# The first norm row spread by four short products, and four instruction orders moved in the token mixers

## The reference, cut to what matters

```python
h = rms_norm(x, norm_mix_pre[l])
z = h @ w_in[l]
q_h, f_fw, f_bw, i_h, g_h, q_d, k_d, v_d, gate_a, gate_b = split(z)
a = hgrn2_mixer(q_h, f_fw, f_bw, i_h, g_h, lb[l], hgrn_gnorm[l])   # 4 heads, gated linear attention, both directions
b = diff_attention(q_d, k_d, v_d, ...)                              # 4 heads, softmax(q k) twice, rope, rms_norm
m = sigmoid(gate_a) * (a @ w_branch_a[l]) + sigmoid(gate_b) * (b @ w_branch_b[l])
x = x + rms_norm(m @ w_out[l], norm_mix_post[l])
x = x + rms_norm(conv_ffn(rms_norm(x, norm_ffn_pre[l]), ...), norm_ffn_post[l])
x = x + rms_norm(sigmoid(rms_unit(x) @ w_ple_gate[l]) * (p[l] @ w_ple[l]), norm_ple[l])
```

## Time and profile before

| what | value |
|---|---|
| median of 3 runs | 2416.17 us (2415.14 to 2419.05) |
| the profiled execution | 2415.63 us, its span 2413.7 us |
| PE busy | 2401.1 us, 99% |
| DVE busy | 1839.3 us, 76% |
| ACT busy | 1311.3 us, 54% |
| POOL busy | 197.1 us, 8% |
| HBM, mean over the span | 132 GB/s |

### The profile page before, as it was taken

How to read it: one execution, slowest core, us unless ns; L and a number is a source line. 1 busy time by engine, 2 the same in 40 slices (tenths; PEclk the granted TensorE clock), 3 DMA queues, 4 the chain that set the end, 5 groups by cost and what they waited for, 6 DMA issues and landing times.

```text
span 2413.7 us, 40388 instructions
## 1 busy us (share of the span) xinstructions
PE 2401.1 (99%) x16188; PEld 2241.4 (93%) x16188; DVE 1839.3 (76%) x2412; ACT 1311.3 (54%) x2022; POOL 197.1 (8%) x236
## 2 busy tenths in 40 slices
PE   9999999999999999999999999999999999999998
PEld 8999999998999999888889999999989999998887
DVE  7666788764888999978585568887649889999784
ACT  6445666542555556456464456664426555554563
POOL 1001011100200000003110011111001000000031
PEclk9999999999999999999999999999999999999999
DMA  5454444353323233733233544434443233346421
GB/s 178 136 175 141 137 146 136 126 181 133 103 89 92 83 97 121 289 123 122 98 131 129 186 136 141 138 129 143 159 150 105 65 90 93 104 164 241 160 89 62
DMA packets 284667, 320.97 MB, mean 133 GB/s; under 512 B 10433, under 2 KB 216769, under 8 KB 284482
## 3 DMA queue, kind: packets, MB, share of 16 engines
q1 hardware_dynamic: 211680, 171.39, 22.8%
q10 hardware_dynamic: 72802, 147.01, 16.8%
HBM read 253.08 MB, written 65.27 MB: 132 GB/s over the span
## 4 chain that ended last, share of the span: by engine, by line
PE 94%; DVE 3%; ACT 1%; issue 1%; DMA 0%; SPq 0%; DVEq 0%; ACTq 0%; POOLq 0%; POOL 0%
PE ps L909 23%; PE ps L1192 14%; PE ps L1397 13%; PE ps L1137 8%; PE ps L882 6%; PE ps L1503 5%; PE ps L1120 3%; PE ps L1366 3%; PE ps L1333 3%; PE ps L896 3%; PE ps L1252 3%; PE ps L961 1%; PE ps L1483 1%; PE ps L1109 1%; PE ps L1089 1%; PE ps L1018 1%
## 5 line engine op out<-in xcount | busy, mean ns | idle before, releaser
L2143 DVE TENSOR_TENSOR wlo<-raw,whi 128x1024 fp32r<-128x1024 f32 (+1 forms) x152 | 163.8, 1079 | 55.1 <-ACT whi L3165 55.1
L909 PE MATMUL ps<-hT_hi,whi 128*128 128x384 f32 x608 | 203.1, 334 | 0.0
L909 PE MATMUL ps<-hT_hi,wlo 128*128 128x384 f32 x608 | 203.1, 334 | 0.0
L909 PE MATMUL ps<-hT_lo,whi 128*128 128x384 f32 x608 | 203.1, 334 | 0.0
L3179 ACT ACTIVATE U<-ps 128x384 f32<-128x384 f32 x152 | 74.8, 492 | 223.2 <-PE ps L909 223.2
L1397 PE MATMUL ps<-whi,PH_hi 128*128 128x512 f32 x456 | 179.0, 393 | 0.0
L1397 PE MATMUL ps<-whi,PH_lo 128*128 128x512 f32 x456 | 177.6, 390 | 0.0
L1397 PE MATMUL ps<-wlo,PH_hi 128*128 128x512 f32 x456 | 177.5, 389 | 0.0
L1584 DVE TENSOR_TENSOR wlo<-raw,whi 128x2048 fp32r<-128x2048 f32 x53 | 121.3, 2288 | 64.8 <-ACT whi L2463 64.8
L1711 DVE TENSOR_TENSOR wlo<-raw,whi 128x1024 fp32r<-128x1024 f32 (+1 forms) x98 | 102.8, 1069 | 79.3 <-ACT whi L2637 79.2
L909 PE MATMUL ps<-S_hi,whi 128*128 128x384 f32 x456 | 152.3, 334 | 0.0
(11 more groups left out here) (348 smaller groups left out, 6940.1 us busy)
## 6 DMA issues: line engine op xcount, KB each, us to landing
raw<-w_up_dram SPq DMA_DIRECT2D x88, 512.0 KB
raw<-w_in_dram SPq DMA_DIRECT2D x62, 512.0 KB
raw<-w_down_dram SPq DMA_DIRECT2D x60, 512.0 KB, 4.5
raw<-w_in_dram SPq DMA_DIRECT2D x16, 1024.0 KB
zT<-gst ACTq DMA_DIRECT2D x40, 384.0 KB, 2.4
GT<-zT ACTq DMA_DIRECT2D x16, 768.0 KB, 5.7
pD<-CG ACTq DMA_DIRECT2D x26, 384.0 KB, 2.3
zT<-hn ACTq DMA_DIRECT2D x48, 192.0 KB, 1.9
```

The source lines that it names most:

```text
L909: ins = mm(ps[:, 4 * (j % 2) + bank, 0:TH], quarter(L, W[y], j, (w,))[:, 0, k * P:(k + 1) * P], sum_operand(a, x, k), start=(opens and k = ...
L2143: v.tensor_tensor(lo, x, hi.bitcast(F32), ALU.subtract)\
```

## The change: what it does

- The first norm row is loaded as four quarters onto partitions 0, 32, 64 and 96. Four products of 256 columns, one on each row group of the array, write it to four banks. ACT copies columns 0 to 511 out and DVE the rest. `WARM` goes from (7, 9, 7) to (5, 12, 7).
- The three small loads of layer constants leave ACT's list ahead of the first table load and come behind the split of the last x tile.
- **Low parts:** on DVE the low parts of slot k (k = 1 to 6) come between queries k and weights k, one step later than before: ahead of the weights of tile k+1 and behind keys, maximum, queries and masked copy of step k.
- **Table:** at the end of a head ACT loads the exponential table and copies the projection of slot 11 before it merges the next head's keys.
- **Diagonal's copy:** in head 0 ACT copies the diagonal out before it issues the store of unit 14.
- **Gate silu:** the next head's gate silu goes from step 5 to step 6, behind that step's projection copy.

```diff
-WARM = (7, 9, 7)
+WARM = (5, 12, 7)
...
-            for i in range(2):
-                ins = mm(ps[:, 1 + i, :], gst[1][0:1, 4 * P:5 * P], wrows[0:1, 1, i * 512:(i + 1) * 512], start=True, stop=True)
+            for i in range(4):
+                ins = mm(ps[:, 1 + i, 0:256], gst[1][i * QR:i * QR + 1, 4 * P:5 * P], wrows[i * QR:i * QR + 1, 1, 0:256], start=True, stop=True)
...
-            v.tensor_copy(wrows[:, 0, :].rearrange("p (b c) -> p b c", b=2), ps[:, 1:3, :]).then_inc(row_copied, 1)
+            v.tensor_copy(wrows[:, 0, 512:D].rearrange("p (b c) -> p b c", b=2), ps[:, 3:5, 0:256]).then_inc(row_copied, 1)
...
                         for t in range(TAIL, len(SLOTS[h - 1])):
                             for j in side_splits(h - 1, t):
                                 low(unit(L, j))
+                    elif k:
+                        side(k)
                     if k + 1 < NT:
                         att_weights(it, k + 1)
-                    side(1 + k)
+                side(NL)
...
-                    dve.wait_ge(row_copied, 1)
+                    dve.wait_ge(row_copied, 2)
...
                 a(Qb[:], FZ[:, 0, :], ACT.Silu).then_inc(*G_gate.step("silu_q"))
+
+            def gla_silu_gate(it):
                 act.wait_ge(s_g, it * 16 + 16)
                 a(gT[:, it % 2, :], gT[:, it % 2, :], ACT.Silu).then_inc(*G_gate.step("silu_g"))
...
                 if h == 0:
                     gla_diagonal(it)
+                    store_out(L, I1, 1)
                 side(PRE)
                 for k in range(NL):
                     side_out(1 + k)
+                    if following and k == NL - 1:
+                        gla_silu_gate(it + 1)
...
+                exponential_table(it)
+                side_out(TAIL + 3)
                 if following:
                     merge_keys(it + 1, 0)
-                exponential_table(it)
                 side(TAIL + 2)
-                side_out(TAIL + 3)
...
-                else:
-                    act.dma_start(wrows[0:1, 1, :], n_mix_pre[0:1, :]).then_inc(row_ld, 16)
...
-            layer_rows(0)
+            act.dma_start(wrows[0:P:QR, 1, 0:256], n_mix_pre[0:1, :].rearrange("o (b c) -> (o b) c", b=4)).then_inc(row_ld, 16)
             for L in range(DEPTH):
                 if L == 0:
                     first_squares(L, 0)
+                    act.wait_ge(row_turned, 1)
+                    a(wrows[:, 0, 0:512].rearrange("p (b c) -> p b c", b=2), ps[:, 1:3, 0:256], ACT.Copy).then_inc(row_copied, 1)
...
                     first_raw(L, 5)
+                    layer_rows(L)
...
                 gla_silu(L * NH)
+                gla_silu_gate(L * NH)
...
                 copy_out(L, I1, 1, (6, 7))
-                store_out(L, I1, 1)
```

More of the change, by code:

```diff
@@ L404, in build @@
         warm_ok = sem("warm_operand_written")
-        row_ld = sem("first_row_on_one_partition")
+        row_ld = sem("first_row_on_four_partitions")
         row_turned = sem("first_row_on_all_partitions")
```

## The result

The changed kernel takes 2422.05 us, the median of 22 runs (2420.53 to 2424.41). The kernel before, beside it on the same chip, takes 2418.11 (2414.85 to 2419.58, 22 runs). The ratio is 1.0020, with a 95% interval of 1.0014 to 1.0026: slower, and by the difference of the medians (3.94 us) inside the 4.8 us, 0.2%, that I had called "the same"; the interval reaches a little beyond. The profiled execution took 2420.57 us, its span is 2418.6, 4.9 more than before.

A forecast was written before the change was run, and what follows sets the result against it. TensorE was taken as the bound, busy 2401.1 of 2413.7 us. The terms -0.5 - 2.4 + 0.2 - 0.7 + 7.3 = +3.9 us led to a forecast of 2419.8 us, range 2412.8 to 2423.5.

The forecast's parts named there:

- the leading case: Whole kernel: a loss inside 0.2% (4.8 us), 2417.5 to 2421.0 us, chance 0.53.
- rival 2: Near products: TensorE waits some 2.7 us, clock falls for 3.4, costing 1.7 us per layer; 2423.2 us, chance 0.28.
- start: Kernel start: scaling up to 1.2 us earlier, only partly arriving; -0.5 us, bounds -1.2 and +1.7.
- the orders on ACT: Mixers: three moves on ACT remove TensorE's waits of 1.2, 0.8 and 0.4 us; -2.4, with +0.2 for head 2.
- low parts but for unit 19's: DVE in the mixers: maximum no longer behind low parts, head 3's late transposed weights gone; -0.7 us.
- unit 19's low part: Head 1: low part ends 3.8 us later, delaying head 2's q and k; +3.65 us per layer, +7.3 in all.
- my upper bound: Start: TensorE's low clock, 3.4 us of it, falls into real products and half is lost; +1.7 us.
- The doubt about head 2: Head 2, step 6: moved gate silu may delay ACT's copy of the states; 0 to 0.25 us per layer, +0.2 taken.
- Head 2: Late weight load ahead of head 3's q and k fits DVE's 2.43 us of idle time; nothing, bounds 0 to +0.8 per layer.

The follow-up runs named there:

- start_only: The kernel before with the start edits alone (row on four partitions, short products, two copies, WARM (5, 12, 7), later small loads): 2416.49 us, ratio 0.9993.
- no_low: The changed kernel with all low parts back in their old order behind the weights: 2414.49 us, ratio 0.9989.
- unit19_back: The changed kernel with only the low part of unit 19 in head 1 back at its old place: 2412.21 us, ratio 0.998.
- filled_wait: The changed kernel with 12 dummy products ahead of TensorE's wait for queries 6 in head 1 of both layers: 2420.86 us.
- low_only: The kernel before with the new order of the low parts alone: 2429.71 us.
- warm_6: qk_first with WARM (5, 6, 7) instead of (5, 12, 7), so 12 dummy instructions instead of 24 ahead of the transposes: 2410.09 us, ratio 0.9969.
- start_7_9_7: The kernel before with the new start but the old WARM (7, 9, 7): 2414.74 us, ratio 0.9988.
- orders_only: The kernel before with the three moves on ACT alone (table, diagonal's copy, gate silu): 2415.78 us, ratio 0.9993.
- qk_alone: The kernel before with one edit, SP issuing the q and k load of head 2 ahead of unit 21: 2417.27 us, ratio 0.9998.
- old_start: The changed kernel with the q and k load of head 2 ahead of unit 21, as in qk_first, and the old start: 2413.36 us.
- qk_first: The changed kernel with SP issuing the q and k load of head 2 ahead of unit 21 instead of behind it: 2411.36 us, ratio 0.9976.

## Why the prediction came out as it did

It said 2419.8 us, range 2412.8 to 2423.5, most likely no difference of 0.2%; 2422.05 lies in the range, and as a ratio the leading case held. As a time it lies 1.05 us beyond that case's own bound of 2421.0, where I had rival 2: my base, a median of three runs, was 2416.17, and beside the change the kernel before takes 2418.11. The +3.9 of the sum and the +3.94 of the medians agree by luck, as errors of both signs cancel. By the differences from the kernel before of four kernels, each with one more of the edits than the one ahead of it (start_only, no_low, unit19_back, the change; they stand in three series):

| term | forecast | measured |
|---|---|---|
| start | -0.5 | -1.6 (in its profile a loss) |
| the orders on ACT | -2.2 | -1.8 (alone -1.7 to -1.8, group by group) |
| low parts but for unit 19's | -0.7 | -2.3 |
| unit 19's low part | +7.3 | +9.6 |

**Unit 19, the main step.** The mechanism was right in every link. Its length can be split by the records of head 1, from the diagonal product to the issue of q and k, from there to the rope product, and from there to the next diagonal:

| kernel, layer | to the issue | to the rope product | to the next diagonal |
|---|---|---|---|
| before, 0 and 1 | 35.41, 35.44 | 10.29, 10.96 | 15.48, 15.26 |
| the change | 38.98, 38.97 | 11.43, 10.92 | 15.72, 15.23 |
| filled_wait | 38.98, 38.97 | 11.96, 11.08 | 15.23, 15.24 |
| low_only | 39.49, 39.50 | 11.65, 13.68 | 17.00, 16.86 |

The first column is the step that I worked out: 3.8 us, measured 3.57 and 3.53. In layer 1 that is all, and the head grew by 3.46, against 3.65. What was mis-sized is the second column, which I had taken as fixed: in layer 0 the transfer took 1.14 us longer from its issue, in `filled_wait` 1.67. The three columns grew by 8.4 us over both layers of the profile; the other 1.2 of the 9.6 are in executions of which there is no profile. I had considered only that it might be quicker behind an idle stretch. ACT's store of `zT` now lies in the middle of it (issued at 341.52, 1.4 us behind that of q and k; before, at 342.29, 5.2 behind), but in layer 1 it does so too and costs nothing, so the store alone doesn't explain it. It is no chance of one profile: in layer 0 the column reads 10.1 to 10.3 in all six profiles with the old place of this low part and the load behind unit 21, and 11.4 to 12.0 in the three with the new one, while in layer 1 the two overlap (10.7 to 11.8, and 10.9, 11.1 and 13.7). The cause is open.

**The clock, rival 2.** The wait and the fall came as that rival has it: 3.51 us of standing still where I had 2.7, the granted clock at 0.5 behind it for 3.4 us ((0.32 + 0.50 + 0.03) x 2 / 0.5 from the windows), in one of two layers of this execution. "TensorE: Matmul & The Clock Gate" of the Trainium skill (Part 1) says that idleness brings the low level back, and the trace agrees: 1.00 until 354, 0.50 behind. In layer 1 it stayed at 1.00 behind 2.99 us. Its price of 1.7 us per layer was wrong here, because the time that TensorE lost lay beside DVE's chain, and the third column grew by 0.2 us only (0.5 against `filled_wait`). In `low_only` the low level lasted 6.8 us in layer 0 (windows of 0.73, 0.50, 0.50 and 0.56, two us each) and the third column grew by 1.5 (1.8 against `filled_wait`): near my number, but for a low level twice as long, so there too about half of its price was hidden. In the median of the change it may hold part of the 1.2 us between it and `filled_wait`; which products were late in the costly executions no trace shows, as none of those was profiled.

**The start.** In the profile the step failed: +0.23 instead of -0.5. I had followed the row, the copies and the scaling (6.45, as forecast) and the second square, but not my own list of what TensorE does meanwhile: 24 dummy instructions of 0.22 us each. `warm_6` and `start_7_9_7` show it, with 12 and 18 of them and a first product at 10.77 and 11.48. The low clock of the earlier trace rows, my upper bound, did not come: the granted clock reads 1.00 from 7 to 11 us. The row's products took 1.24 us where I had 0.5, but they did work side by side: 1024 columns in all take 1.24 us as four of 256 and 3.78 as two of 512, both at the slow rate (the dummies around them take 0.22 to 0.25 us each, later 0.12). "TensorEngine Tiling (Array Packing)" of the Trainium skill, Key Properties, says that different tiles work in parallel, and this agrees. The drain at a change of mode, which it also states, can't be told apart here: the weight loads pause 0.65 us ahead of the dummies, and 0.76 us in the kernel before. In the median the term was won by something that the prediction doesn't have, the late start in half of the executions of the kernel before.

**The orders on ACT.** Right in place, and near in size: their lines are gone, and they gave 1.7 to 1.8 us where I had 2.2. The doubt about head 2 was not needed; its length changed by +0.03 and -0.02 us.

**The other low parts.** Right in direction, three times too small. I sized them by the wait of 0.7 us in the earlier trace rows; but once the orders on ACT are in, the late weights are what ends next, 1.7 us in `no_low` and in `orders_only`, and this order takes these too. That leaves some 0.6 us of its 2.3 without a row.

**Head 2.** q and k of head 3 wait 2.22 and 2.11 us for their transfer now (0.54 and none before), and DVE's idle time behind the rope product swallows it, as forecast.

## What to carry to other kernels

An order in one engine's list is also an order in the queue that waits for it: here 2.3 us of VectorE work, moved behind a maximum that could not start earlier, cost 9.6 us by way of a transfer that has nothing to do with it, and moving that transfer one place up in its queue turned a loss of 3.9 into a gain of 6.5. The edit on the queue alone was worth nothing, so two edits have to be judged together where one releases the other. Before a start is rearranged, look at the times of all runs and not at one profile: two groups of times can be a second path, and dummies that keep an engine busy have to end before the work that they wait for is ready.

## What the hardware showed that I had not expected

- TensorE at the start: the column of the granted clock reads 1.00 in the first 7 us (in the changed kernel all through), but 14 dummies take 3.19 to 3.36 us there and 1.73 us later. The duration is what counts; the column doesn't show this slowness. With the old start, TensorE either was fast for the row's products (1.98 us in the kernel before, 2.12 in `orders_only`) or stayed slow until 12 us (3.78 in `low_only`, `qk_alone` and `old_start`). By the groups of times about half of the executions of the kernel before are of each kind.
- A wait of TensorE of 2.99 us (the change, layer 1) left the clock up; waits of 3.51 (the change, layer 0), 3.74 and 5.76 us (`low_only`) went with the low level.
- Low clock on TensorE is not lost time by itself. 3.4 us of it went with 0.2 to 0.5 us more from the rope product to the next diagonal, where DVE set the head's end, 6.8 us of it (`low_only`) with 1.5 to 1.8.
- The load of q and k took between 8.4 us (`qk_first`: issued 334.89, rope product at 343.27 with no wait, so at most that) and 13.7 us (`low_only`, layer 1) from its issue, with the same bytes of its own. In `qk_first` no weight unit is ahead of it; behind a weight unit the shortest in these profiles is 10.1 us (`no_low`, layer 0).
